# Modulation vectors from weight blocks held stationary in TensorE, in four chunks, with x loaded between them

## The reference, cut to what matters

```python
def adaln(cond, w_ada, b_ada):
    m = jax.nn.silu(cond) @ w_ada + b_ada
    return jnp.split(m, 3, axis=-1)

def hybrid_layer(x, ctx, c, c_ctx, w_ada, b_ada, norm_g, w_in, ...):
    shift, scale, gate = adaln(c, w_ada, b_ada)
    shift_c, scale_c, gate_c = adaln(c_ctx, w_ada, b_ada)
    h = rmsnorm(x, norm_g) * (1 + scale[:, None]) + shift[:, None]
    hc = rmsnorm(ctx, norm_g) * (1 + scale_c) + shift_c
    q, k, v, za, u, bg, cg, zc = jnp.split(h @ w_in, SPLIT_POINTS, axis=-1)
```

## Time and profile before

| | us |
|---|---|
| median of 3 runs | 2445.01 |
| lowest and highest of the 3 | 2443.3, 2446.46 |
| the profiled execution, its own time | 2442.55 |
| its span in the trace | 2440.8 |
| PE busy in the span | 2386.9 |

### The profile page before, as it was taken

How to read it: one execution, slowest core, us unless ns; L and a number is a source line. 1 busy time by engine, 2 the same in 40 slices (tenths; PEclk the granted TensorE clock), 3 DMA queues, 4 the chain that set the end, 5 groups by cost and what they waited for, 6 DMA issues and landing times.

```text
span 2440.8 us, 33800 instructions
## 1 busy us (share of the span) xinstructions
PE 2386.9 (98%) x12072; PEld 1992.7 (82%) x12072; DVE 1459.6 (60%) x2338; ACT 954.1 (39%) x1761; POOL 984.2 (40%) x776
## 2 busy tenths in 40 slices
PE   7999999999999999999999999999999999999998
PEld 3888888887888888888888788877877888888886
DVE  5865656477454445445454653445586656798878
ACT  4443434344133444434534521234243333444443
POOL 1323132222482222222222233311366666698785
PEclk9999999999999999999999999999999999999999
DMA  9413132223453221222122244311314444644442
GB/s 326 155 37 122 35 107 59 86 71 123 139 185 101 83 60 59 69 84 74 52 74 78 91 138 164 103 44 44 103 44 149 162 156 147 233 157 163 147 147 86
DMA packets 87145, 271.92 MB, mean 111 GB/s; under 512 B 10057, under 2 KB 10185, under 8 KB 82001
## 3 DMA queue, kind: packets, MB, share of 16 engines
q1 hardware_dynamic: 64560, 184.37, 22.9%
q10 hardware_dynamic: 22432, 85.60, 10.9%
HBM read 198.08 MB, written 58.23 MB: 105 GB/s over the span
## 4 chain that ended last, share of the span: by engine, by line
PE 88%; DVE 8%; issue 1%; ACT 1%; POOL 0%; DMA 0%; DVEq 0%; SPq 0%; POOLq 0%; ACTq 0%
PE ps L2967 12%; PE ps L2969 12%; PE ps L2968 11%; PE ps L3720 8%; PE ps L3729 8%; PE ps L3722 7%; PE ps L2983 4%; PE ps L2985 4%; PE ps L2987 4%; PE ps L3432 3%; PE ps L3234 2%; PE ps L3210 1%; PE ps L3553 1%; PE ps L3529 1%; PE ps L3578 1%
## 5 line engine op out<-in xcount | busy, mean ns | idle before, releaser
L733 POOL CAST w_hi<-raw 128x1024 fp32r<-128x1024 f32 x112 | 120.2, 1074 | 1074.9 <-issue 365.3
L2967 PE MATMUL ps<-act_hi,w_hi 128*128 128x512 f32 x1248 | 498.9, 400 | 1.9 <-DVE act_lo L2609 1.1
L2969 PE MATMUL ps<-act_hi,w_lo 128*128 128x512 f32 x1248 | 488.6, 391 | 0.0
L2968 PE MATMUL ps<-act_lo,w_hi 128*128 128x512 f32 x1248 | 486.8, 390 | 0.0
L735 POOL TENSOR_TENSOR w_lo<-raw,w_hi 128x1024 fp32r<-128x1024 f32 x112 | 281.5, 2514 | 9.0
L2969 PEld LDWEIGHTS ps<-act_hi,w_lo 128*128 128x128 f32 x1248 | 234.2, 188 | 51.9
L2967 PEld LDWEIGHTS ps<-act_hi,w_hi 128*128 128x128 f32 x1248 | 234.6, 188 | 45.1 <-DVE act_lo L2609 1.5
L2968 PEld LDWEIGHTS ps<-act_lo,w_hi 128*128 128x128 f32 x1248 | 234.9, 188 | 40.7
L2983 PE MATMUL ps<-act_hi,w_hi 128*128 128x512 f32 x384 | 151.0, 393 | 5.6 <-DVE act_lo L1901 4.0
L2985 PE MATMUL ps<-act_lo,w_hi 128*128 128x512 f32 x384 | 150.3, 391 | 0.0
L2987 PE MATMUL ps<-act_hi,w_lo 128*128 128x512 f32 x384 | 118.6, 390 | 0.0
(11 more groups left out here) (546 smaller groups left out, 5823.7 us busy)
## 6 DMA issues: line engine op xcount, KB each, us to landing
raw<-in_w_stream_dram SPq DMA_DIRECT2D x192, 512.0 KB, 3.6
x_own_f<-a_dram SPq DMA_DIRECT2D x32, 512.0 KB, 5.2
a_dram<-stage SPq DMA_DIRECT2D x18, 512.0 KB, 6.2
ada<-in_w_ada_dram SPq DMA_DIRECT2D x4, 2048.0 KB, 17.1
spill<-res ACTq DMA_DIRECT2D x16, 512.0 KB, 5.0
gate_dram<-gate_sb ACTq DMA_DIRECT2D x32, 256.0 KB, 2.0
stage<-spill ACTq DMA_DIRECT2D x16, 512.0 KB, 4.0
act_lo_f<-a_dram SPq DMA_DIRECT2D x16, 512.0 KB, 5.3
```

The lines of the kernel that those rows point to most:

```text
L733: nc.gpsimd.tensor_copy(w_hi[:, s, :, :], raw[:, s, :, :]).then_inc(S["w_hi"], 1)
L2967: nc.tensor.matmul(out, wh, xh, start=start, stop=False, skip_group_check=onto)
L2968: nc.tensor.matmul(out, wh, xl, start=False, stop=False, skip_group_check=onto)
L2969: return nc.tensor.matmul(out, wl, xh, start=False, stop=stop, skip_group_check=onto)
```

## The change

The weights of the modulation become the stationary operand, in blocks of 128 by 128, and the condition (`silu`, two columns) the moving one, so that the result comes out with one value per partition and nothing has to be turned. The host lays `w_ada` out anew (`_modulation`): chunk j holds, for the operand rows 2j and 2j+1, shift and scale. PE computes a chunk in `modulated(j)` with 32 matmuls in plain float32 (2 rows, shift and scale, 8 blocks each). DVE turns each row's result into `mod` and `gs` with two small operations (`modulation(k)`). `ada_plain`, `ada_parts`, `turn_rows`, `ada_hi`, `ada_lo` and `ada_row` go. Between the chunks stand pairs of matmuls whose result nobody reads (`clock_kept`). Loads are in a new order; the squares go to `act_lo_f`, one buffer a row; and chunks 2 and 3 stand behind the spread and inside the first rows.

```diff
+            def ada_load(j):
+                sp.dma_start(ADA_SLOT[j].rearrange("p a m k c -> p (a m k c)"), w_ada[j]).then_inc(S[ADA_IN[j]], 16)
+            def x_load(j):
+                sp.dma_start(res[:, 2 * j:2 * j + 2, :], x_t[:, 2 * j:2 * j + 2, :]).then_inc(S[X_IN[j]], 16)
             ada_load(0)
+            x_load(0)
+            x_load(1)
             ada_load(1)
-            sp.dma_start(res[:, 0:4, :], x_t[:, 0:4, :]).then_inc(S["x_in"], 16)
+            x_load(2)
+            x_load(3)
+            tile_load(0)
+            tile_load(1)
             ada_load(2)
             ada_load(3)
-            sp.dma_start(res[:, 4:6, :], x_t[:, 4:6, :]).then_inc(S["kv_in"], 16)
-            sp.dma_start(res[:, 6:8, :], x_t[:, 6:8, :]).then_inc(S["x_rest"], 16)
-            tile_load(0)
-            tile_load(1)
-            sp.wait_ge(S["ada_used"], 2)
+            sp.wait_ge(S["ada_turned"], 2)
             sp.dma_start(ctxT[:, :, :], ctx_r).then_inc(S["rows_in"], 16)
...
+            sp.wait_ge(S["ada_turned"], 6)
+            for m in range(2, 6):
+                gate_load(m)
+            sp.wait_ge(S["ada_turned"], 8)
+            for m in range(2):
+                gate_load(m)
...
-            pool.wait_ge(S["acc_done"], 8)
             split(0, 0, free=False)
...
+            for k in range(KT):
+                act.wait_ge(S[X_IN[k // 2]], 16)
+                nc.scalar.activation(act_lo_f[:, k, :], res[:, k, :], ACT.Square).then_inc(S["sq_ready"], 1)
             norm_rms("x0")
...
+            def modulation(k):
+                dve.wait_ge(S["ada_turned"], k + 1)
+                nc.vector.tensor_scalar(out=mod[:, k, :], in0=mod_rows(0, k), scalar1=vec[:, V_BADA + k:V_BADA + k + 1],
+                                        scalar2=None, op0=ALU.add).then_inc(S["ada_step"], 1)
+                nc.vector.tensor_scalar(out=gs[:, k, :], in0=mod_rows(1, k), scalar1=mod[:, 8 + k, 0:1],
+                                        scalar2=vec[:, V_NORM + k:V_NORM + k + 1], op0=ALU.add, op1=ALU.mult
+                                        ).then_inc(S["ada_step"], 1)
...
+            for k in range(0, KT, 2):
+                for m in {2: (4, 5), 6: (6, 7)}.get(k, ()):
+                    modulation(m)
+                x_scaled(k)
+                x_scaled(k + 1)
+                x_low(k)
+                if k == KT - 2:
+                    norm_rstd("ctx")
+                x_low(k + 1)
...
+            def clock_kept(n):
+                for _ in range(n):
+                    nc.tensor.matmul(bank(7), ident, con[:, 0:BANK], start=True, stop=True)
+            def modulated(j):
+                pe.wait_ge(S[ADA_IN[j]], 16)
+                for m in range(2):
+                    if j == 3:
+                        pe.wait_ge(S["ada_step"], 10 + 2 * m)
+                    for a in range(2):
+                        for k in range(KT):
+                            last = nc.tensor.matmul(mod_rows(a, 2 * j + m), ADA_SLOT[j][:, a, m, k, :], silu[:, k, :],
+                                                    start=(k == 0), stop=(k == KT - 1))
+                    last.then_inc(S["ada_turned"], 1)
+            pe.wait_ge(S["small_in"], 48)
+            clock_kept(2)
+            pe.wait_ge(S["c_sig"], 2)
+            modulated(0)
+            clock_kept(2)
+            modulated(1)
+            clock_kept(2)
             sum_squares("x0")
             spread("x0")
+            modulated(2)
...
             for k in range(4):
                 first_rows(0, [k])
                 first_rows(1, [k])
+                if k == 1:
+                    modulated(3)
+            first_rows(0, range(4, 6))
+            pe.wait_ge(S["ada_step"], 2 * KT)
             spread("ctx")
-            first_rows(0, range(4, KT)).then_inc(S["tile_done"], 1)
+            first_rows(0, range(6, KT)).then_inc(S["tile_done"], 1)
```

More of the change, by code:

```diff
@@ L1932, in _ @@
[L1932 to L1943, removed]
@@ L1945, in _ @@
-            for k in range(4):
-                accumulate("x0", k, stage[:, k % 2, :])
-            ada_lo(2)
-            ada_lo(3)
-            for k in range(4, 8):
-                accumulate("x0", k, stage[:, k % 2, :])
-            dve.drain().then_inc(S["acc_done"], 8)
-            dve.wait_ge(S["ada_turned"], 4)
-            rows = bank(4, 0, 64).rearrange("p (m j) -> p m j", j=4)
-            nc.vector.tensor_copy(mod[:, 0:16, :], rows[:, :, 2:4]).then_inc(S["ada_step"], 1)
-            dve.wait_ge(S["ada_step"], 1)
@@ new lines, in _ @@
+            dve.wait_ge(S["const_ready"], 4)
+            for k in range(4):
+                accumulate("x0", k, act_lo_f[:, k, :])
+            modulation(0)
+            modulation(1)
+            for k in range(4, KT):
+                accumulate("x0", k, act_lo_f[:, k, :])
+            dve.drain().then_inc(S["acc_done"], 8)
+            modulation(2)
+            modulation(3)
+            norm_rstd("x0")
+            dve.wait_ge(S["rstd_spread"], 1)
+            for k in range(0, KT, 2):
[7 more added lines that the diff above has]
+                x_low(k + 1)
@@ L2229, in _ @@
             dve.drain()
-            dve.wait_ge(S["ada_step"], 12)
+            dve.wait_ge(S["ada_step"], 24)
             def add_square(name, norm, s, i):
@@ L3023, in spread @@
                 last.then_inc(S["rstd_spread"], 1)
-            def ada_plain(n, rows):
-                pe.wait_ge(S[ADA_IN[n]], 16)
-                for k in range(rows):
-                    last = nc.tensor.matmul(ps[0:4, n * BANK:(n + 1) * BANK], cond4[:, k, :], ADA_SLOT[n][:, k, :],
-                                            start=(k == 0), stop=(k == KT - 1))
-                return last
-            def ada_parts(n):
-                out = ps[0:4, n * BANK:(n + 1) * BANK]
-                for j in range(2):
-                    pe.wait_ge(S["lo_ready"], 8 * (n - 2) + 4 * j + 4)
-                    for k in range(2):
-                        x = slice(k * BANK, (k + 1) * BANK)
-                        for part in (act_hi, act_lo):
-                            last = nc.tensor.matmul(out, cond4r[:, 2 * j + 4 + k, :], part[:, 2 * (n - 2) + j, x],
-                                                    start=False, stop=(j == 1 and k == 1 and part is act_lo))
-                last.then_inc(S["ada_used"], 1)
@@ L3046, in turn_rows @@
-            def turn_rows(n):
-                pe.wait_ge(S["ada_rows"], n + 1)
-                for m in range(4):
-                    last = nc.tensor.transpose(bank(4, 16 * n + 4 * m, 16 * n + 4 * m + 4),
-                                               mrow[:, n % 2, m * P:(m + 1) * P], ident[0:4, 0:4])
-                last.then_inc(S["ada_turned"], 1)
-            pe.wait_ge(S["c_sig"], 4)
-            ada_plain(0, KT).then_inc(S["ada_used"], 1)
-            ada_plain(1, KT).then_inc(S["ada_used"], 1)
@@ L3085, in context_keys @@
                 return project(s, 6, hc_hi, hc_lo, C, ready=filled("ctx"))
-            pe.wait_ge(S["ada_step"], 4)
+            pe.wait_ge(S["ada_step"], 2 * KT)
             def out_step(s, j):
@@ L3940 @@
                band_t=_place_rpb(a["rpb"][0]), strip_t=_place_rel(a["rel_bias_2"]), w_fl=w_fl,
-               w_ada=_tiles(a["w_ada"][0][:, :2 * D], BANK),
+               w_ada=_modulation(a["w_ada"][0]),
                w_gate=a["w_ada"][0][:, 2 * D:].T.reshape(KT, P, D), w_stream=w_stream)
```

102 lines of the change are left out of this document (32 added, 70 removed).

## The result

| | us |
|---|---|
| changed kernel, median of 4 runs | 2472.12 (2471.51 to 2474.12) |
| kernel before, median of 4 runs | 2444.44 (2443.3 to 2446.46) |
| ratio | 1.0114, 95% interval 1.0096 to 1.0131 |
| the profiled executions, after and before | 2474.12, 2442.55 |

The change makes the kernel 1.1% slower, 27.7 us by the medians and 31.6 us between the two profiled executions; that of the changed kernel was the slowest of its four runs, that of the kernel before was faster than all four of its own. It was forecast as slower, 2468.5 us in a range from 2456 to 2477.

The account below looks back on a forecast made before the run. PE, busy 98% of the span, was taken to bound the kernel; 12.4 + 9.0 + 2.0 = 23.4 us later made 2466.0 on the profiled execution's 2442.55, 2468.5 for the median, range 2456 to 2477.

Parts of the forecast that it names:

- such work doesn't hold the clock: Chunks: two-column matmuls with nothing wide between run at half clock, 0.21 us a record, 13.4 us a chunk.
- The rival in which the full clock holds through the chunks: Opening: narrow matmuls keep the clock as wide ones do, 2.8 us faster in all, 2442.2; chance 0.18.
- The rival of cheaper narrow records: Chunks: a half-clock record costs less than double, say 0.15 us, 9.6 a chunk; about 13 us slower, 2458; chance 0.09.
- chunk 0: Opening, from piece 0's landing at 10.4: at half clock until 23.8, 13.4 us.
- pair: Between chunks: two 512-column matmuls, 3.4 us at half clock or 1.7 at full, which may or may not raise the clock.
- chunk 1: Behind the second pair: 13.4 us if the clock stayed down, 9.0 if raised; the middle taken, 11.2.
- first product at: End of the opening, behind chunk 2: first product starts at 61.6 instead of 49.21, 12.4 us later.
- chunk 3: Behind rows 0 and 1: full clock for 4.4 us, then half, 9.0 us; bounds 6.7 and 13.4.
- half clock behind it: Products of rows 2 on, behind chunk 3: 3.9 us needed to raise the clock, at half pace, 2.0 us later.
- later at the end of the rows: Sum for the opening and first rows: 12.4 + 9.0 + 2.0 = 23.4 us later.
- no pair raises it: Slow bound of the main case: chunk 2 until 65.1, 15.9 us later, 31.3 in all, 2476.3.
- What was hidden: First rows and context: DVE's small operations, `hc_lo`, gate loads and POOL's split were claimed to stay off PE's path.

Follow-up runs that it names:

- e2: Changed kernel with four wide matmuls at the start and two more behind every eight narrow ones; four runs at 2467.22, 2481.61, 2494.52 and 2496.15 us.
- e7: Changed kernel with chunk 3's narrow matmuls in four groups of eight among products of rows 2 and 3; 2467.6 us, 1.008 of the kernel before.
- e4: Changed kernel with half of the narrow matmuls left out (64 of 128); 2445.67 us, 1.0002 of the kernel before.
- e3: Changed kernel with chunks 2 and 3 moved ahead of the sum of squares; 2477.07 us, 1.0133 of the kernel before.
- e5: Changed kernel with the condition stationary again, the weights moving 512 columns wide, and wide fillers in opening gaps; 2445.31 us, 1.0000 of the kernel before.
- e9: Changed kernel with four wide matmuls at the start and four behind every eight narrow ones; 2494.91 to 2504.44 us.
- e1: Changed kernel without its three pairs of clock-keeping matmuls; 2465.69 us, 1.0088 of the kernel before.

## Why the prediction was right, and where its sum was short

*The direction and the mechanism.* The step "such work doesn't hold the clock", read from the earlier trace rows, is what the runs show: e2's fast execution and e7's groups have the narrow matmuls at 0.105 us a record with the clock at full, the changed kernel, e4 and e7's chunks 0 to 2 at 0.21 to 0.22 with it at half. The rival in which the full clock holds through the chunks (2442) failed: from 10.4 on PE was busy but for 0.66 us, and the chunks still ran at the half-clock price. The rival of cheaper narrow records failed as well: twice the full-clock price was right to within 0.4 us a chunk.

*Term by term*, by the changed kernel's chain and timeline:

| term | forecast | measured |
|---|---|---|
| chunk 0 | 13.4 | 13.8 |
| pair | 3.4 | 3.6 |
| chunk 1 | 11.2 | 13.4 |
| pair | 3.4 | 3.6 |
| sum of squares | 2.6 | 3.2 |
| root, reciprocal | 0.6 | 0.7 |
| spread | 3.2 | 3.8 |
| chunk 2 | 13.4 | 13.5 |
| first product at | 61.6 | 65.9 |
| rows 0 and 1, against before | 0 | +0.6 |
| chunk 3 | 9.0 | 9.9 |
| half clock behind it | 2.0 | about 2 |
| later at the end of the rows | 23.4 | 29.3 |

The term most mis-sized is the one taken in the middle: that a pair raises the clock every second time. In this trace neither did, which gives the bound worked out as "no pair raises it": 65.1 for the first product, measured 65.9. That alone is 2.2 us in chunk 1 and 1.2 in the sum and the spread. In e3 both pairs did raise it, so the middle was no mistake of mechanism, but over these four runs (2471.5 to 2474.1) the time lies at the slow side of the range. The rest is small: a narrow record is 0.21 to 0.215 at half clock, the wide record of a pair 0.9, and in chunk 3 the full clock lasted 3.8 us where 4.4 were taken, which makes 9.9 of 9.0.

All the larger errors go one way. The sum for the profiled execution was 2466.0, and it took 2474.12, 8.1 us more: 5.9 in the opening, 2.3 behind it. That the median forecast is only 3.6 us short (2468.5 for 2472.12) owes something to luck, namely to which executions were profiled.

*What was hidden stayed hidden.* Between rows PE didn't wait for DVE: the low parts of rows 2 and 3 were there at 71.5, before chunk 3 began, and those of rows 4 and 5 at 76.4 (the prediction had all four made during the chunk), row 6's was there at 88.2 and row 7's at 90.6, and PE's records follow each other without a gap from 83.7 on. The loads were in time, `hc_lo` was done at 103.4 and read at 109 or later. One cost was hidden that the prediction had not seen: with POOL's split no longer held back until the squares were summed, both ran together. DVE's timeline, the last two of four additions:

```profile
27.44 1.87 DVE L1848 TENSOR_TENSOR acc0b<-acc0b,act_lo_f 128x1024 f32<-128x1024 f32 x1
29.41 3.18 DVE L1848 TENSOR_TENSOR acc0b<-acc0b,act_lo_f 128x1024 f32<-128x1024 f32 x1
```

and POOL's:

```profile
28.31 3.21 POOL L744 TENSOR_TENSOR w_lo<-raw,w_hi 128x1024 fp32r<-128x1024 f32 x1
```

The two additions ahead of them took 1.23 each, the first before POOL had started (26.65) and the second beside the head of its cast; all four took 7.82 us here and 5.22 before, and the subtraction took 2.38 before. The sum was ready at 32.6 and PE wanted it at 44.9, so it cost nothing. In e5, whose chunks are at full clock, DVE's additions are on the path, and the last one took 1.87 beside the same subtraction.

*Behind the opening* nothing was forecast, and 2.3 us came in the profiled execution. From tile 2's first matmul to the end of the trace it is 2367.5 us in the kernel before and 2369.7 in the changed one, and from 2367.0 (e2) to 2370.6 (e9) in the profiled executions of the experiments, so single executions differ there by more than these 2.3 us. The fall of the clock at 719.5 doesn't account for it: e2 and e5 have such a fall and are the shortest there (2367.0, 2367.2), e1 has none and took 2368.8. What makes this scatter stays open.

## What to carry to other kernels

Count what a reorientation does to the moving side: 32 matmuls of two columns and eight of 512 cost about the same at full clock (6.7 and 6.96 us here), but in these traces only the wide ones kept the clock; the narrow ones lost it within their own chunk, paid double from then on and handed a half-speed engine to what followed. Narrow matmuls that can't be avoided belong in small groups between wide ones that the kernel needs anyway (e7), not in one piece, and a burst of useless wide work ahead of them is no cure: it cost 3.6 us and gave back about 3 where it worked at all. An engine that shows 100% busy can still be at half clock: read the durations of its records and the granted clock beside the busy share.

## What the runs showed that I had not expected

- The same pair of wide matmuls (3.6 us) raised the clock in one execution (e3, chunk 1 in 10.35 us) and not in another (13.44), and e2's four runs lay 29 us apart. A design that depends on whether the clock comes up is uneven as well as slower.
- A spread of 16 records with 128 moving columns (3.8 us at half clock) was enough in e1 for the clock to rise behind it, so that chunk 2 took 10.35, and in e4 as well; in the changed kernel it was not.
- Two of DVE's additions took 1.87 and 3.18 us beside POOL's subtractions and casts instead of 1.23, and POOL's subtraction 3.21 instead of 2.38.
